# A one-core two-block transformer layer on Trainium2: first units behind three norms in halves of the tokens, and a re-ordered cross attention

## The reference

```python
# block 1
h = rms_norm(x, norm_g); mem_h = rms_norm(mem, mem_norm_g)          # x 512x1024, mem 256x1024
(c_glu, c_gate, d_q, d_k, d_v, d_gate, x_q, x_gate, merge) = split(h @ w_in)
y_conv = conformer_conv_branch(c_glu, c_gate, ...)                   # 31 taps, layer norm
y_diff = differential_attention_branch(d_q, d_k, d_v, d_gate, ...)   # 8 heads
# cross attention: 4 heads of 256
k, v = split(mem_h @ w_mem_kv)
q, k = rms_norm(q, qn_g), rms_norm(k, kn_g)
y_mem = (softmax(q @ k.T * 256**-0.5) @ v * silu(x_gate)) @ w_x_proj
x = x + (sigmoid(merge_0)*y_conv + sigmoid(merge_1)*y_diff + sigmoid(merge_2)*y_mem) @ w_out
# block 2
x = layer_norm(x, emb_ln); h = x * (1 + sc1) + sh1                   # "emb"
p = h @ w_in_2                                                       # pu, pv, then the rwkv columns
mix = concat(gmlp_spatial_gating(pu, pv), rwkv7_time_mix(...)) @ w_out_2
x = layer_norm(ALPHA * x + gt1 * mix, ln1); h = x * (1 + sc2) + sh2  # "ln1"
f = (silu(h @ w_g) * (h @ w_u)) @ w_ffn_out
x = layer_norm(ALPHA * x + gt2 * f, ln2)
```

## Time and profile before

| | |
|---|---|
| median of the runs | 1663.46 us (1661.16 to 1664.08) |
| the profiled execution, device time | 1662.28 us |
| its span, first to last instruction | 1660.5 us |
| TensorE matmul busy | 1576.3 us, 95% |
| TensorE weight load busy | 1254.0 us, 76% |
| VectorE / ScalarE / GpSimd busy | 995.2 / 722.5 / 190.9 us |
| mean granted TensorE clock | 0.988 of full speed |

### The profile page before, as it was taken

How to read it: one execution, slowest core, us unless ns; L and a number is a source line. 1 busy time by engine, 2 the same in 40 slices (tenths; PEclk the granted TensorE clock), 3 DMA queues, 4 the chain that set the end, 5 groups by cost and what they waited for, 6 DMA issues and landing times. The chain is left out here.

```text
span 1660.5 us, 24142 instructions
## 1 busy us (share of the span) xinstructions
PE 1576.3 (95%) x9852; PEld 1254.0 (76%) x9852; DVE 995.2 (60%) x1676; ACT 722.5 (44%) x1159; POOL 190.9 (11%) x159
## 2 busy tenths in 40 slices
PE   6999999999999999899999898988998999999997
PEld 5877776788788767676788687767766887888886
DVE  4999985556555476657444647776547353334445
ACT  6543367245523476557622535554424322223112
POOL 2443465400010000000005000000000000000000
PEclk9999999999999999999999999999998999999999
DMA  5232243654464322232334232200012332323331
GB/s 208 93 97 77 78 152 103 204 155 138 136 191 154 114 90 89 67 99 77 114 102 135 70 115 76 77 28 4 4 39 66 113 115 89 101 91 100 90 100 51
DMA packets 45645, 166.07 MB, mean 100 GB/s; under 512 B 5264, under 2 KB 5392, under 8 KB 45536
## 3 DMA queue, kind: packets, MB, share of 16 engines
q1 hardware_dynamic: 42912, 155.95, 29.6%
q0 software_dynamic: 2624, 8.59, 1.8%
HBM read 162.42 MB, written 2.10 MB: 99 GB/s over the span
## 5 line engine op out<-in xcount | busy, mean ns | idle before, releaser
L569 PE MATMUL bank<-h_T_hi,weight_hi 128*128 128x512 f32 x1208 | 488.2, 404 | 8.4 <-DVE conv_in L2102 3.2
L604 ACT ACTIVATE weight_hi<-raw 128x1024 fp32r<-128x1024 f32 x241 | 254.7, 1057 | 549.4 <-PE bank L571 541.0
L612 DVE TENSOR_TENSOR weight_lo<-raw,weight_hi 128x1024 fp32r<-128x1024 f32 x184 | 225.6, 1226 | 432.6 <-ACT weight_hi L604 432.6
L571 PE MATMUL bank<-h_T_hi,weight_lo 128*128 128x512 f32 x1208 | 477.2, 395 | 0.0
L570 PE MATMUL bank<-h_T_lo,weight_hi 128*128 128x512 f32 x1208 | 476.5, 394 | 0.0
L569 PEld LDWEIGHTS bank<-h_T_hi,weight_hi 128*128 128x128 f32 x1208 | 229.5, 190 | 65.8 <-issue 9.9
L570 PEld LDWEIGHTS bank<-h_T_lo,weight_hi 128*128 128x128 f32 x1208 | 229.3, 190 | 51.7 <-issue 3.9
L571 PEld LDWEIGHTS bank<-h_T_hi,weight_lo 128*128 128x128 f32 x1208 | 228.7, 189 | 50.0
L2105 DVE SCALAR_TENSOR_TENSOR bank<-conv_in,columns,bank 128x512 f32<-128x512 f32 x240 | 181.4, 756 | 8.3
L612 POOL TENSOR_TENSOR weight_lo<-raw,weight_hi 128x1024 fp32r<-128x1024 f32 x57 | 139.5, 2448 | 182.6 <-ACT weight_hi L604 182.6
L570 PE MATMUL bank<-branch_lo,weight_hi 128*128 128x512 f32 x192 | 75.5, 393 | 0.0
(11 more groups left out here) (448 smaller groups left out, 2266.5 us busy)
## 6 DMA issues: line engine op xcount, KB each, us to landing
raw<-in_weights SPq DMA_DIRECT2D x289, 512.0 KB, 3.5
x_in<-in_x SPq DMA_DIRECT2D x4, 512.0 KB, 5.5
x_rows<-in_x POOLq DMA_DIRECT2D x4, 512.0 KB, 4.9
out<-x_rows SPq DMA_DIRECT2D x4, 512.0 KB, 2.6
mem_in<-in_mem POOLq DMA_DIRECT2D x2, 512.0 KB, 8.0
ln_rows<-in_ln_g POOLq DMA_DIRECT2D x4, 256.0 KB, 4.1
ln_rows<-in_ln_b POOLq DMA_DIRECT2D x4, 256.0 KB, 4.7
silu_row<-in_c POOLq DMA_DIRECT2D x1, 512.0 KB, 11.1
```

Of the source, the lines that this page charges most:

```text
L569: pe.matmul(o, lhs[0], rhs[0], start=start, stop=False)
L571: return pe.matmul(o, lhs[1], rhs[0], start=False, stop=stop)
L604: act.activation(parts[n % SPLIT][0][:, :], raw[u % RAW][:, :], ACT.Copy).then_inc(*weight_hi.up(u))
L612: engine.tensor_tensor(lo[:, :], raw[u % RAW][:, :], view(hi[:, :]), ALU.subtract).then_inc(*ready.up(u))
```

## The change

- At the start ScalarE loads the table for exp and ln before anything waits, VectorE squares and sums rows 1 and 3 while ScalarE does 0 and 2, the loads of `mem` and `c` wait until the third weight unit has landed, and `pe_first_unit` runs `conv_b 0` in halves of 256 tokens between the transposes of group 1.
- At emb and ln1, `first_units` runs the first two units (`pu 0` and `pu 1`, `ffn_g 0` and `ffn_u 0`: `EARLY`) in halves: four steps of group 0's tokens for both units, then the turns of group 1, then the other four steps, then group 1's tokens. These four units leave the ring of three: each has a pair of tiles of its own in memory that is free by then. Their `hi` and `lo` are made before the norm begins, the next ones during and behind it.
- In cross attention VectorE adds the two tiles of squares (`add_squares`) and `query_sum` is one matmul instead of two. ScalarE takes `x_gate 0` and squares `xq 0` inside the loop of the convolution branch's silu. The last head's first value moves behind step 2 and its second into the middle of step 3.

```diff
+EARLY = (("pu", 0), ("pu", 1), ("ffn_g", 0), ("ffn_u", 0))
...
-    turn_of = {u: n for n, u in enumerate(weights_of)}
+    in_turn = [u for u in weights_of if plan[u][0] not in EARLY]
+    turn_of = {u: n for n, u in enumerate(in_turn)}
...
-            if n >= SPLIT:
-                act.wait_ge(*given_back(weights_of[n - SPLIT]))
-            act.activation(parts[n % SPLIT][0][:, :], raw[u % RAW][:, :], ACT.Copy).then_inc(*weight_hi.up(u))
+            if plan[u][0] == EARLY[0]:
+                act.wait_ge(*y_lo.at(KT - 1))
+            elif plan[u][0] == EARLY[2]:
+                act.wait_ge(*yb_lo.at(FW - 1))
+            elif plan[u][0] not in EARLY and turn_of[u] >= SPLIT:
+                act.wait_ge(*given_back(in_turn[turn_of[u] - SPLIT]))
+            act.activation(weight_parts(u)[0][:, :], raw[u % RAW][:, :], ACT.Copy).then_inc(*weight_hi.up(u))
...
+        pool.wait_ge(*raw_loaded[2].at(2))
         for t in range(MT):
             pool.dma_start(mem_in[t][:, :], dram["mem"][cut(t), :]).then_inc(*mem_loaded[t].up())
...
+    def first_units(pe, what, labels, rhs):
...
+        use = [(unit_bank(pe, label), weight_parts(index[label])) for label in labels]
...
+        def products(g, features):
+            tokens = turned_columns(g)
+            for k in features:
+                pe.wait_ge(*turned_lo.at(what, g, k))
+                for label, (bank, (hi, lo)) in zip(labels, use):
+                    done = mm3(pe, bank[:, tokens], (hi[:, cut(k)], lo[:, cut(k)]), (rhs[0][:, k, tokens], rhs[1][:, k, tokens]),
+                               k == 0, k == KT - 1)
...
+        products(0, range(KT // 2))
+        pe_turn_group(pe, what, x_rows, 1)
+        products(0, range(KT // 2, KT))
+        products(1, range(KT))
...
+    def pe_first_unit(pe, label):
...
+        for pair in range(KT // 2):
+            pe_turn_pair(pe, "x", x_in, 1, pair)
+            if pair == 0:
+                pe.wait_ge(*lo_ready(index[label]))
+            for k in (2 * pair, 2 * pair + 1):
+                products(0, k)
+        for k in range(KT):
+            done = products(1, k)
...
-            for c in range(2):
-                pe.wait_ge(*norm_sq.at("xq", h, c))
-                done = pe.matmul(bank, ones_all[:, :], norm_ring_q["xq", h, c], start=c == 0, stop=c == 1)
-            done.then_inc(*norm_sum.up("xq", h))
+            pe.wait_ge(*squares_added.at(h))
+            pe.matmul(bank, ones_all[:, :], norm_ring_q["xq", h, 0], start=True, stop=True).then_inc(*norm_sum.up("xq", h))
...
-        middle = {0: first_scores, 1: first_turns, 2: lambda: pe_cross_value(pe, h - 1, 0)}
+        middle = {0: first_scores, 1: first_turns, 3: second_value}
...
     def pe_second_in(pe):
-        pe_turn_group(pe, "emb", x_rows, 1)
-        for n in range(4):
-            feature_unit(pe, ("pu", n), unit_bank(pe, ("pu", n)), h2_T,
-                         ready=(lambda k: turned_lo.at("emb", 1, k)) if n == 0 else None)
+        first_units(pe, "emb", EARLY[0:2], h2_T)
+        for n in range(2, 4):
+            feature_unit(pe, ("pu", n), unit_bank(pe, ("pu", n)), h2_T)
...
     def act_program(act):
+        exp_table(act)
         act.wait_ge(*consts.at())
-        for t in range(TT):
+        for t in (0, 2):
             act_square_rows(act, "x", t, x_in[t], x_loaded[t])
+            act.wait_ge(*row_squared.at(t + 1))
+            act_root_rows(act, "x", t + 1)
...
+            if n == 4:
+                act_x_gate(act, 0)
+            if n == 6:
+                act_query_square(act, 0, 0)
...
     def act_first_out(act):
         act_y_hi(act, KT - 1)
-        feed_hi(act, KT - SPLIT)
+        feed_hi(act, KT - SPLIT + 2)
...
+        for t in (0, 2):
+            dve_square_rows(dve, "x", t + 1, x_in[t + 1], x_loaded[t + 1])
+            dve_root_rows(dve, "x", t, x_in[t])
+            dve_root_rows(dve, "x", t + 1, x_in[t + 1])
...
+        def add_squares(h):
...
+            dve.tensor_tensor(norm_ring_q["xq", h, 0], norm_ring_q["xq", h, 0], norm_ring_q["xq", h, 1], ALU.add).then_inc(
+                *squares_added.up(h))
...
-        feed_lo(dve, KT // 2 - SPLIT)
+        feed_lo(dve, KT // 2 - SPLIT + 2)
         dve_rows(dve, "emb", h2_T, lambda t: residual(t, 1))
```

More of the change, by code:

```diff
@@ L404, in build @@
     y_b = here("y_b", [P, FW, 2, S], FP32R)
+    here, there = Map(nc, Y_AT, H_AT), Map(nc, B_AT, M_AT)
+    early_parts = {label: (here if n < 2 else there).pair(f"early_weight{n}", [P, UNIT]) for n, label in enumerate(EARLY)}
     here = Map(nc, H_AT, B_AT)
@@ L592, in given_back, with weight_parts @@
         return product.at(*label)
+    def weight_parts(u):
+        return early_parts[plan[u][0]] if plan[u][0] in EARLY else parts[turn_of[u] % SPLIT]
     def feed_hi(act, count=1):
@@ L1455, in pe_ffn @@
     def pe_ffn(pe):
-        pe_turn_group(pe, "ln1", x_rows, 1)
-        for n in range(FT):
+        first_units(pe, "ln1", EARLY[2:4], h3_T)
+        for n in range(1, FT):
             if n == 10:
                 pe_gate_rows(pe, 5)
-            feature_unit(pe, ("ffn_g", n), unit_bank(pe, ("ffn_g", n)), h3_T,
-                         ready=(lambda k: turned_lo.at("ln1", 1, k)) if n == 0 else None)
+            feature_unit(pe, ("ffn_g", n), unit_bank(pe, ("ffn_g", n)), h3_T)
             feature_unit(pe, ("ffn_u", n), unit_bank(pe, ("ffn_u", n)), h3_T)
@@ L1658, in act_keys, with act_x_gate, act_query_square @@
                 values(1)
+            if n == 4:
+                act_x_gate(act, 0)
+            if n == 6:
+                act_query_square(act, 0, 0)
         act_branch_hi(act, "conv", KT - 1, silu_ring[KT - 1], conv_gated.at(KT - 1))
+    def act_x_gate(act, n):
+        act_take(act, ("x_gate", n), x_gate_ring.take(act, n, branch_lo, "cross", n), ACT.Silu)
+    def act_query_square(act, h, c):
+        o = norm_ring_q.take(act, ("xq", h, c), norm_lo, "xq", h, c)
+        act.wait_ge(*product.at("xq", 2 * h + c))
+        act.activation(o, units["xq", 2 * h + c], ACT.Square).then_inc(*norm_sq.up("xq", h, c))
     def act_cross(act):
@@ L1672, in turns @@
             act.activation(p_T[0][:, :, cut(t)], grid(side["xt", h, t][:, 0:M]), ACT.Copy).then_inc(*p_hi.up("x", h, t))
-        def squares(h):
-            for c in range(2):
-                o = norm_ring_q.take(act, ("xq", h, c), norm_lo, "xq", h, c)
-                act.wait_ge(*product.at("xq", 2 * h + c))
-                act.activation(o, units["xq", 2 * h + c], ACT.Square).then_inc(*norm_sq.up("xq", h, c))
         def query_hi(h):
@@ L1685, in query_hi @@
                 act.activation(q_x[h % 2][0][:, c, :], norm_ring_q["xq", h, c], ACT.Copy).then_inc(*norm_hi.up("xq", h, c))
-        def gate(h, c):
-            n = 2 * h + c
-            act_take(act, ("x_gate", n), x_gate_ring.take(act, n, branch_lo, "cross", n), ACT.Silu)
         def gated_hi(h, c):
@@ L1706, in act_cross @@
                 exps(h - 1, 3)
+                act_query_square(act, h, 0)
                 turns(h - 1, 0)
                 turns(h - 1, 1)
+            act_query_square(act, h, 1)
             if h == 0:
-                gate(h, 0)
+                exp_table(act)
                 feed_hi(act)
-                exp_table(act)
-            feed_hi(act)
-            squares(h)
+                feed_hi(act)
             if later:
@@ L1721, in act_cross @@
                 feed_hi(act)
-                gate(h, 0)
+                act_x_gate(act, 2 * h)
             if later:
@@ L1725, in act_cross @@
             feed_hi(act)
-            gate(h, 1)
+            act_x_gate(act, 2 * h + 1)
             if later:
@@ L1745, in act_cross @@
                     turns(h - 1, t)
-            if step == 2:
+            if step == 3:
                 gated_hi(h - 1, 0)
@@ L2115, in dve_turned, with dve_square_rows @@
               view(pair[0][:, k, turned_columns(g)]), ALU.mult, ALU.subtract).then_inc(*turned_lo.up(what, g, k))
+    def dve_square_rows(dve, what, t, source, loaded):
+        dve.wait_ge(*loaded.at())
+        dve.scalar_tensor_tensor(out=dve_junk, in0=source[:, :], scalar=1.0, in1=source[:, :], op0=ALU.mult, op1=ALU.mult,
+                                 accum_out=spot(what, "sq", t)).then_inc(*row_squared.up(t))
     def dve_root_rows(dve, what, t, source):
@@ L2259, in turns @@
                      p_hi.at("x", h, t)).then_inc(*p_lo.up("x", h, t))
+        def add_squares(h):
+            for c in range(2):
+                dve.wait_ge(*norm_sq.at("xq", h, c))
+            dve.tensor_tensor(norm_ring_q["xq", h, 0], norm_ring_q["xq", h, 0], norm_ring_q["xq", h, 1], ALU.add).then_inc(
+                *squares_added.up(h))
         def query_full(h):
```

72 lines of the change are left out of this document (44 added, 28 removed).

## The result

The changed kernel takes **1647.3 us** (median of 4 runs, 1646.42 to 1648.18) against 1663.77 of the kernel before beside it: ratio 0.9902, 95% interval 0.9888 to 0.9916. The profiled execution took 1646.84 us with a span of 1645.0 us, where the earlier trace rows has 1660.5.

A forecast was written before the change was run, and what follows sets the result against it. TensorE, computing 1576.3 of 1660.5 us, was taken as the bound, so time comes from its gaps and slow or needless matmuls. Gains 2.1 + 7.0 + 4.3 + 3.3 = 16.7 us gave 1646.8 us, range 1641.5 to 1655.5.

The forecast's parts named there:

- Start, 2.1: Kernel start: earlier roots and first unit in halves bring `conv_a 0` from 27.77 to 25.7, 2.1 us gained.
- Cross attention, 7.0: Cross attention: three edits together gain 7.0 us, or 4.0 if one of (a) and (b) is hidden.
- (a): Cross attention, heads 1 to 3: one sum matmul less saves 0.85 us per head, 2.55 us together.
- (b): Cross attention, head 0: with the gate taken early, `proj 0` starts at 292.0 instead of 294.68, 2.7 us gained.
- (c): Cross attention, last head: its value, moved half a unit later, no longer waits for probabilities, 1.75 us gained.
- Emb, 4.3: Emb norm: early weights and filling halves gain 4.3 us, between 5.0 with the clock up and 2.0 with it down.
- Ln1, 3.3: Ln1 norm: the same edits gain 3.3 us with the clock low until 1285.7, between 5.2 and 1.0.
- The bounds: Whole kernel: the terms' bounds added, gains of 20.8 us giving 1642.7 and of 7.0 us giving 1656.5.
- A: Rival at start and norms: halves run at 1.2 GHz, later row chain eats the rest; 9.0 us gained, 1654.5; chance 0.2.
- C: Rival in cross attention: VectorE's add and head 0's root come late; 2 of 7.0 us gained, 1651.8; chance 0.08.
- D: Rival behind emb and ln1: clock stays at 1.2 GHz in the units there; 41 us slower, 1704; chance 0.02.
- B: Rival on the clock: never falls at the norms, rises early at the start; 20.0 us gained, 1643.5; chance 0.17.

## Why the prediction was right

The forecast was 1646.8 us; 1647.3 were measured. Point by point:

- **Start, 2.1:** 2.07, `conv_a 0` at 25.70 as said, and the clock rose at 21.3, near the 21.1 of the working. That it did so in the first profile is partly luck. In the ten profiles with this start `conv_a 0` lies between 24.2 and 26.1, 1.7 to 3.6 us sooner than the 27.8 before, mostly by when the clock rose (at 18.4 us in the soonest, at 21.3 to 21.6 in the four latest); the first turn began at 8.2 to 9.6.
- **Cross attention, 7.0:** 7.38. (a) was 2.55; the shift grows by 0.87, 0.84 and 0.84 us in heads 1 to 3. (b), put at 2.7, was 2.8. (c), put at 1.75, was 2.0. Taking (a) back cost 2.66. Ahead of `proj 0` TensorE now stands idle for 1.01 us, but it starts where the working had it (291.9 in the time of the kernel before, said 292.0).
- **Emb, 4.3:** 5.0. The working with the clock up was right to 0.1 us: counted from the first turn (8.36 us sooner than before), TensorE lost 0.74 ahead of group 0 (said 0.8), group 1's turns ended at 936.3 (927.94 + 8.36; said 936.4), and `pu 2` came at 945.02 (936.66 + 8.36; said 945.0). **What failed is the choice between its ends**: I took 4.3, between 5.0 with the clock up and 2.0 with it down, and it stayed up in all nine profiles with a fill or with transposes. By the rule of the Trainium skill that the prediction names, emb would have given 2.0. This trace doesn't agree with it, and neither does the run with transposes in the gap.
- **Ln1, 3.3:** 4.5. Idle time (2.68, said 2.9) and transposes were as said. The clock was back at 1270.7, which is 1281.7 in the time of the kernel before, instead of at 1285.7. It was that term's length of the slow stretch that was mis-sized, against this profile. But the 4.5 contain luck: the slow stretch of the first profile of the kernel before was 10.2 us long, and 3.4 in the second. First turn to `ffn_g 1` took 29.15 us in the first and 28.38 to 28.40 in the three other profiles that have the old norms; 24.64 and 25.39 in the two of the change. So ln1 gains 3.0 to 3.8 us as a rule, and 3.3 was a good figure. (The working itself adds up to 1291.4, not 1291.1, which is 3.0.)
- **A term that was missing:** 3.4 us given back where nothing was changed. I had put the way between the edited places at nothing. Of it, 1.1 us were a low stretch of that one execution. The other 2.35 came again as 2.0 in the second profile and cannot be put down to the clock's coming and going; why is open. Gains that were larger than their terms by 2.3 us in these two profiles, and this omission, met, which is why the sum hit the median to 0.5 us; that closeness is partly luck. The median is 16.2 to 16.5 us lower by two comparisons.
- **The bounds:** the terms at their best add up to 20.0 us (1643.5), and not to the 20.8 of the prediction, for which it shows no terms; its low sum of 1656.5 lies outside its own range, which ends at 1655.5. Neither bears on the outcome.
- **Rivals:** A, C and D fell. The case of B came true at emb alone. What "would show it" held, save that the first full unit behind ln1 came 15.5 us sooner and not 16.7, and that a wait of 0.23 us for VectorE's addition stands ahead of head 0's sum (the sign of C, but only in this head).

## What to carry to other kernels

When an engine waits for the first rows of a norm, give it the part of the next product that needs only the rows that are there. The gain is that work itself (here 2.9 of 3.7 us at emb), and the clock is the smaller part. Where TensorE's work ahead can't be had, a string of throw-away transposes in a wait whose PSUM bank it already owns held the clock up at three places here. At the key sum it cost nothing: `pu 2` to the key sum took 82.93 us with 36 transposes and 83.01 without. At ln1, 24 transposes that left 2.94 us of idle time behind them did not hold it. And before a few us in one profile are explained by an edit, profile the same kernel again: the windows of low clock must be booked separately, by what they do to the way between two fixed matmuls, since the matmul time lost in them is more than the path pays (2.5 against 0.8 us at ln1).

## What the runs showed of the hardware

- Which waits bring the clock down differs from execution to execution. Behind the 3.08 us wait of the dv unit the clock was at the lower level from 683.6 us in one execution of the changed kernel, and never in the next one. In the kernel before it fell 4.5 us after TensorE had gone idle there, in the change 2.2 us after. The Trainium skill (TensorE: Matmul & The Clock Gate, Part 1) says that the number of slow matmuls varies from run to run of one kernel; it says so of the start. These traces agree there (the clock rose between 18.4 and 21.6 us in the ten profiles with the changed start) and show it in mid-kernel too.
- With transposes in the wait the granted clock stayed at the upper level at emb (24; one profile), at the key sum (36; two profiles) and at ln1 (22 and 14; one profile each). The Trainium skill (TensorE: Matmul & The Clock Gate, "Part 4: PE-mode transpose") says that they don't count as matmuls do; these three places don't agree. Whether they can raise a low clock is not shown: at the start it rose only once halves ran between them.
- GpSimd and VectorE, both at work in SBUF, held each other up: 0.69 became 2.62 us for one VectorE instruction with two inputs in SBUF, while GpSimd took 5.67 us for its two subtractions there, 4.84 at emb. The Trainium skill (SBUF — State Buffer, Terms) says that the two share a pair of ports, and that the loser is blocked for the whole of the other's instruction. 2.62 - 0.69 = 1.9 us is less than the 2.46 us of one subtraction, so the trace agrees with that.
